# Where the squares of a norm, its scaling, its turns by feature halves, and the feed-forward sums stand in a two-block kernel

## The reference, cut to what matters

```
def rms_norm(x, g):
    y = xf * lax.rsqrt(jnp.mean(xf * xf, axis=-1, keepdims=True) + EPS)
    return (y * g.astype(jnp.float32)).astype(x.dtype)
...
# first block, every layer
h = _rms(x, norm_g[l]);  proj = h @ w_in[l]
dots = jnp.einsum('bqhd,bsd->bqhs', iqb, ik) * IDX_HD ** -0.5
score = jnp.einsum('bqhs,bqh->bqs', jax.nn.relu(dots), iwb)
...
x = x + merged @ w_out[l]
...
# second block, every layer
h = rms_norm(x, norm1) * (1.0 + scale1) + shift1
proj = h @ w_in
...
x = x + gate1 * mix
h2 = rms_norm(x, norm2) * (1.0 + scale2) + shift2
ff = jnp.square(jax.nn.relu(h2 @ w_ff1)) @ w_ff2
return x + gate2 * ff
```

## Time and profile before

| | |
|---|---|
| median of 3 executions | 2875.72 us (2864.07 to 2878.76) |
| profiled execution | 2862.72 us, span 2860.8 us |
| TensorE products busy | 2559.2 us, 89% of the span |
| VectorE / ScalarE / GpSimd busy | 1437.6 / 945.9 / 877.4 us |
| mean granted TensorE clock | 0.947 of full speed |

### The profile page before, as it was taken

How to read it: one execution, slowest core, us unless ns; L and a number is a source line. 1 busy time by engine, 2 the same in 40 slices (tenths; PEclk the granted TensorE clock), 3 DMA queues, 4 the chain that set the end, 5 groups by cost and what they waited for, 6 DMA issues and landing times. The chain is left out here.

```text
span 2860.8 us, 34637 instructions
## 1 busy us (share of the span) xinstructions
PE 2559.2 (89%) x12407; PEld 2036.8 (71%) x12407; DVE 1437.6 (50%) x2989; ACT 945.9 (33%) x1725; POOL 877.4 (31%) x366
## 2 busy tenths in 40 slices
PE   5998999889999898988988778999997877899999
PEld 4786777677778686767876446878787654787877
DVE  4396343565449634365464555444557455533234
ACT  3333243432333324343233452322223354232221
POOL 2232423224323241423432002444433200244442
PEclk9898999999989999999999789999998888999999
DMA  4222423225422241413432002444433200223232
GB/s 139 73 82 59 143 71 112 65 62 171 134 74 85 78 142 50 125 45 96 173 97 70 1 1 59 140 133 147 151 124 91 66 1 1 59 89 103 89 96 80
DMA packets 133583, 256.01 MB, mean 89 GB/s; under 512 B 23406, under 2 KB 30124, under 8 KB 133420
## 3 DMA queue, kind: packets, MB, share of 16 engines
q1 hardware_dynamic: 133420, 253.81, 28.4%
HBM read 249.58 MB, written 4.19 MB: 89 GB/s over the span
## 5 line engine op out<-in xcount | busy, mean ns | idle before, releaser
L693 POOL TENSOR_TENSOR wl<-raw,wh 128x1024 fp32r<-128x1024 f32 (+2 forms) x362 | 877.2, 2427 | 1955.8 <-ACT wh L1070 1954.1
L763 PE MATMUL ps<-wh,hTh 128*128 128x512 f32 (+4 forms) x1664 | 668.5, 402 | 14.6 <-DVE hTl L1624 14.6
L1070 ACT ACTIVATE wh<-raw 128x1024 fp32r<-128x1024 f32 (+2 forms) x362 | 379.8, 1049 | 864.8 <-PE ps L763 444.5
L763 PE MATMUL ps<-wl,hTh 128*128 128x512 f32 (+4 forms) x1664 | 649.7, 390 | 0.0
L763 PE MATMUL ps<-wh,hTl 128*128 128x512 f32 (+4 forms) x1664 | 649.2, 390 | 0.0
L763 PEld LDWEIGHTS ps<-wh,hTh 128*128 128x128 f32 x1664 | 329.0, 198 | 85.3 <-issue 29.8
L763 PEld LDWEIGHTS ps<-wh,hTl 128*128 128x128 f32 x1664 | 328.1, 197 | 60.5
L763 PEld LDWEIGHTS ps<-wl,hTh 128*128 128x128 f32 x1664 | 329.1, 198 | 53.1
L717 PE MATMUL ps<-cf,arena 128*128 128x128 f32 x800 | 135.5, 304 | 136.1 <-DVE arena L1983 24.2
L763 PE MATMUL ps<-hTh,wh 128*128 128x512 f32 (+1 forms) x672 | 250.0, 372 | 6.3 <-DVE hTl L1624 5.1
L763 PE MATMUL ps<-hTh,wl 128*128 128x512 f32 (+1 forms) x672 | 248.9, 370 | 0.0
(11 more groups left out here) (265 smaller groups left out, 3297.5 us busy)
## 6 DMA issues: line engine op xcount, KB each, us to landing
raw<-in_w_in_dram SPq DMA_DIRECT2D x160, 512.0 KB, 3.6
raw<-in_w_ff_dram SPq DMA_DIRECT2D x128, 512.0 KB, 3.6
modw<-in_w_mod_dram SPq DMA_DIRECT2D x96, 512.0 KB, 4.6
raw<-in_w_br_dram SPq DMA_DIRECT2D x24, 512.0 KB, 3.7
raw<-in_w_out_dram SPq DMA_DIRECT2D x24, 512.0 KB, 3.7
xm<-in_x_dram SPq DMA_DIRECT2D x8, 512.0 KB, 4.6
raw<-in_w_out_dram SPq DMA_DIRECT2D x16, 256.0 KB, 3.9
raw<-in_w_in_dram SPq DMA_DIRECT2D x8, 408.0 KB, 3.2
```

What stands on the lines that cost most here:

```text
L693: pool.tensor_tensor(piece(wl, g % RING, u), piece(raw, g % RING, u), piece(wh, g % SPLIT, u).bitcast(F32), ALU.subtract)\
L763: last = pe.matmul(*args, start=(q == 0 and c == 0 and n_pass == 0), stop=(q == u["quarters"] - 1 and c == u["chunks"] - 1 and n_pass == 2))
L1070: act.activation(piece(wh, g % SPLIT, u), piece(raw, g % RING, u), ACT.Copy)\
```

## The change

It has these parts, all in one build:

1. In a norm head with sweeps in front, the squares of tiles 0 and 1 stand ahead of the first of the last four sweeps and no longer behind it.
2. ScalarE scales the even tile of a pair, VectorE only the odd one.
3. The two tiles of a pair are turned by feature halves: half 0 of both tiles through VectorE and ScalarE first, then half 1.
4. Results that went from PSUM to `scr` and were used from there stay in their PSUM bank (relu of the indexer, `mix`, `fu`, `br`), which is marked free one operation later or more.
5. The feed-forward's sum is multiplied by the gate at group 6 of 0 to 7 and added to `xm`, and group 7 is multiplied and added by itself: three operations a slice at group 6 and two at group 7, where it was one and three.
6. The bias of the attention is one or two `tensor_scalar` of one column each.
7. As `mod` steps avoid sweeps beside a norm head, nearly all of them move by one sweep.

```diff
-            line.extend(last[0:1] + stats(0) + last[1:3] + two("turn", 0) + last[3:4] + stats(1))
+            line.extend(stats(0) + last[0:3] + two("turn", 0) + last[3:4] + stats(1))
...
                 elif kind == "turn":
                     _, stage, t = step
-                    pe.wait_ge(dve_result, at("xn", stage, t))
+                    pe.wait_ge(act_result if t % 2 == 0 else dve_result, at("xn", stage, t))
...
+                elif kind == "scale":
+                    _, stage, pair = step
+                    act.wait_ge(dve_result, at("root", step))
+                    act.activation(xn[:, 0], xm[:, 2 * pair], ACT.Copy, scale=nsm[:, 3, 0:1])\
+                        .then_inc(act_result, mark(act_result, ("xn", stage, 2 * pair)))
...
-                    act.activation(scratch(("scr", step))[:, 0:WIDTH[t]], ps[:, bank_of.get(step, 0), 0:WIDTH[t]], ACT.Relu)\
-                        .then_inc(act_result, mark(act_result, ("relu", step), ("free", step)))
+                    b = ps[:, bank_of.get(step, 0), 0:WIDTH[t]]
+                    act.activation(b, b, ACT.Relu).then_inc(act_result, mark(act_result, ("relu", step)))
...
-                    dve.tensor_tensor(tmp, b, tmp, ALU.mult).then_inc(dve_result, mark(dve_result, ("relu2", i, s), free))
+                    dve.tensor_tensor(b, b, tmp, ALU.mult).then_inc(dve_result, mark(dve_result, ("relu2", i, s), ("free", key)))
                     dve.wait_ge(dve_result, now(dve_result))
                     dve.wait_ge(act_result, at("fh", i, s))
-                    dve.tensor_tensor(F[g % 2][1][:, idx, t0:t0 + n], tmp, F[g % 2][0][:, idx, t0:t0 + n].bitcast(F32), ALU.subtract)\
-                        .then_inc(dve_result, mark(dve_result, ("free", key), *([] if mode == "feat0" else [("f", l, g, idx)])))
+                    dve.tensor_tensor(F[g % 2][1][:, idx, t0:t0 + n], b, F[g % 2][0][:, idx, t0:t0 + n].bitcast(F32), ALU.subtract)\
+                        .then_inc(dve_result, mark(dve_result, free, *([] if mode == "feat0" else [("f", l, g, idx)])))
...
-                    if g < FF_GROUPS - 1:
+                    if g < FF_GROUPS - 2:
                         dve.tensor_tensor(acc, b, acc, ALU.add).then_inc(dve_result, mark(dve_result, free))
                         dve.wait_ge(dve_result, now(dve_result))
                         return
...
+                    if g == FF_GROUPS - 2:
+                        dve.tensor_tensor(b, b, acc, ALU.add).then_inc(dve_result, mark(dve_result))
+                        dve.wait_ge(dve_result, now(dve_result))
+                    dve.tensor_tensor(b, b, grow2[:, c * 512:(c + 1) * 512], ALU.mult).then_inc(dve_result, mark(dve_result))
...
+                    dve.wait_ge(dve_result, at("guess", step, 3, 0))
+                    dve.tensor_scalar(nsm[:, 3, 0:1], y[:, 0:1], -1.0 / 8192.0, None, ALU.mult)\
+                        .then_inc(dve_result, mark(dve_result, ("root", step)))
+                    t = 2 * pair + 1
+                    dve.wait_ge(dve_result, at("guess", step, 3, 1))
+                    dve.tensor_scalar(xn[:, t % 2], xm[:, t], y[:, 1:2], -1.0 / 8192.0, ALU.mult, ALU.mult)\
+                        .then_inc(dve_result, mark(dve_result, ("xn", stage, t)))
...
-                    key = ("scr", step)
+                    key = step
                     W = WIDTH[t]
                     dve.wait_ge(act_result, at("relu", step))
-                    r = scr[:, scr_slot[key], 0:W]
+                    r = ps[:, bank_of.get(step, 0), 0:W]
```

More of the change, by code:

```diff
@@ L355, in build @@
                 kind = u["name"]
-                if kind in ("bq", "bk", "cq", "ck", "bz", "cz", "gz", "ek", "eq") or kind[:4] in ("gate", "mix0", "mix1") \
-                        or kind[:2] == "fu" or kind[:3] == f"fd{FF_GROUPS - 1}":
+                if kind in ("bq", "bk", "cq", "ck", "bz", "cz", "gz", "ek", "eq") or kind[:4] == "gate" \
+                        or kind[:2] == "fu":
                     keys = [("scr", i, 2 * p), ("scr", i, 2 * p + 1)]
-        elif step[0] == "index" or (step[0] == "y_tok" and step[2] != "c"):
+        elif step[0] == "y_tok" and step[2] != "c":
             keys = [("scr", step)]
@@ L1428, in evacuate @@
                     dst = xm[:, idx, c * 512:(c + 1) * 512]
[L1429 removed]
                     dve.wait_ge(product, at("product", i, s))
                     dve.wait_ge(act_result, at("grow", l, 0))
[L1432 to L1435 removed]
+                    dve.tensor_tensor(b, b, grow[:, c * 512:(c + 1) * 512], ALU.mult).then_inc(dve_result, mark(dve_result))
                     dve.wait_ge(dve_result, now(dve_result))
[L1437 to L1438 removed]
+                    dve.tensor_tensor(dst, b, dst, ALU.add)\
+                        .then_inc(dve_result, mark(dve_result, free, *([("x", ("f", l), idx)] if c else [])))
                 elif name[:2] == "fu":
@@ L1596, in _ @@
                                 .then_inc(dve_result, mark(dve_result, ("guess", step, r + 1, k)))
-                    for k in range(2):
-                        t = 2 * pair + k
-                        dve.wait_ge(dve_result, at("guess", step, 3, k))
-                        dve.tensor_scalar(xn[:, t % 2], xm[:, t], y[:, k:k + 1], -1.0 / 8192.0, ALU.mult, ALU.mult)\
-                            .then_inc(dve_result, mark(dve_result, ("xn", stage, t)))
+                    dve.wait_ge(dve_result, at("guess", step, 3, 0))
@@ L1603, in _ @@
                     _, stage, t = step
[L1604 removed]
+                    if t % 2 == 0:
+                        continue
                     for hb in range(2):
[L1606 to L1617 removed]
@@ L1618, in _ @@
-                    if t % 2 == 1:
+                        pair = []
                         for t2 in (t - 1, t):
                             st = ("turn", stage, t2)
-                            tile = slice(t2 * P, (t2 + 1) * P)
-                            for hb in range(2):
-                                dve.wait_ge(act_result, at("hh", st, hb))
-                                dve.tensor_tensor(hTl[:, 4 * hb:4 * hb + 4, tile], h32(st, hb),
-                                                  hTh[:, 4 * hb:4 * hb + 4, tile].bitcast(F32), ALU.subtract)\
-                                    .then_inc(dve_result, mark(dve_result, ("h", stage, t2, hb), ("free", (st, hb))))
+                            v = ps[:, bank_of.get((st, hb), 0)].rearrange("p (c n) -> p c n", c=4)
+                            pair.append((st, t2, v))
+                            dve.wait_ge(product, at("turned", st, hb))
+                            if stage[0] == "n":
+                                g = col("norm_g", stage[1], 4 * hb, 4).unsqueeze(2).to_broadcast([P, 4, P])
+                                dve.tensor_tensor(v, v, g, ALU.mult).then_inc(dve_result, mark(dve_result, ("h32", st, hb)))
+                            else:
+                                lo = (0 if stage[0] == "a" else 24) + 4 * hb
+                                g = gain[:, 0 if stage[0] == "a" else 1, 4 * hb:4 * hb + 4].unsqueeze(2).to_broadcast([P, 4, P])
+                                shift = modT[:, stage[1], lo:lo + 4].unsqueeze(2).to_broadcast([P, 4, P])
+                                dve.tensor_tensor(v, v, g, ALU.mult).then_inc(dve_result, mark(dve_result))
+                                dve.wait_ge(dve_result, now(dve_result))
+                                dve.tensor_tensor(v, v, shift, ALU.add).then_inc(dve_result, mark(dve_result, ("h32", st, hb)))
@@ L1627, in _ @@
+                        for st, t2, v in pair:
+                            tile = slice(t2 * P, (t2 + 1) * P)
+                            dve.wait_ge(act_result, at("hh", st, hb))
+                            dve.tensor_tensor(hTl[:, 4 * hb:4 * hb + 4, tile], v,
+                                              hTh[:, 4 * hb:4 * hb + 4, tile].bitcast(F32), ALU.subtract)\
+                                .then_inc(dve_result, mark(dve_result, ("h", stage, t2, hb), ("free", (st, hb))))
                 elif kind == "rstd":
@@ L1790, in _ @@
                     dve.wait_ge(dve_result, now(dve_result))
-                    dve.scalar_tensor_tensor(s[:, 2:2 + k], s[:, 0:k], -1.0, q_scale(m, t, h), ALU.mult, ALU.mult)\
-                        .then_inc(dve_result, mark(dve_result, ("bias", l, m, n)))
+                    for c in range(k):
+                        ins = dve.tensor_scalar(s[:, 2 + c:3 + c], s[:, c:c + 1], -1.0, q_scale(m, t, h)[:, c:c + 1],
+                                                ALU.mult, ALU.mult)
+                    ins.then_inc(dve_result, mark(dve_result, ("bias", l, m, n)))
                 elif kind == "prob":
```

53 lines of the change are left out of this document (15 added, 38 removed).

## The result

| | before | changed |
|---|---|---|
| median | 2872.51 us (4 executions, 2864.07 to 2878.76) | 2845.07 us (4 executions, 2837.92 to 2848.93) |
| profiled execution | 2862.72 us | 2837.92 us |

The ratio is 0.991, with a 95% interval of 0.9881 to 0.9939: 26 us less, between 18 and 34. A later series of six executions of the same kernel gave 0.9928 (0.9903 to 0.9953), 21 us less. The forecast was 12.7 us less, a time of 2857.6 us; the median of 2845.07 lies outside its own range (2851 to 2865) and inside the whole one (2842 to 2877).

What follows compares the result with a forecast made beforehand. TensorE, busy 2559.2 of 2860.8 us, was taken to set the end. Heads -15.9, indexer +9.7, feed-forward -3.6 and smaller terms sum to -12.7 us, put on the mean 2870.3: 2857.6 us; own range 2851 to 2865, whole 2842 to 2877.

Steps and rivals of the forecast that it cites:

- rival 2: Whole kernel: fewer long waits mean fewer lower-clock sweeps, and less contention; 12 us more gain, 2845 us; chance 0.17.
- The heads: Six norm heads: TensorE's waits at transposes shrink by new timetables, n0 alone gets longer; -15.9 us in all.
- Halves take off another 1.7: Head a1: turning by feature halves saves another 1.7 us, part of that head's -7.8 us.
- ScalarE's wait for the root: Norm heads: it delays roundings of weight pieces by 4 us, but these are wanted later; costed at nothing.
- The indexer: Groups of four dots: the fourth waits until VectorE has read the first bank, not for ScalarE's relu; +9.7 us.
- The feed-forward: Behind each `fu`: the first rest gets faster but its bank is freed later; -0.27 in 14 places, -3.6 us.
- `fd6`: Feed-forward group 6: 16 more operations cost +0.5 us, only in layer 0; bank waits here would show the forecast wrong.
- Slower, by one operand in PSUM being held up: `fu` rests and dot groups: GpSimd holds up operations with one PSUM operand as with two in SBUF; 2891 us; chance 0.04.
- the rule that the prediction weighed: VectorE: a PSUM source costs 120 fixed cycles against 58, an estimated 3 us on the path; the prediction followed the rows instead.
- `mod`, "-2, +0.5": Attention: the 2.90 us step ahead of it runs a sweep earlier, -2 us; another comes before the first attention, +0.5.
- More gaps cost some clock: +1: Indexer's stretch: more gaps in TensorE's work cost some clock, +1 us.
- Bias and `br`, "-1.5": Attention: one-column bias operations and `br` sums with one PSUM operand save 1.5 us on the path (bounds 0 and -5).

Runs made afterwards that it cites:

- experiment 2: The kernel before with only the norm heads' parts (squares first, even tile on ScalarE, turns by halves) and the shift of the mod steps; ratio 0.9965.
- experiment 5: The kernel before with the heads' three parts and the gate at group 6, whose sums stay in PSUM; ratio 0.9919.
- experiment 6: The changed kernel with the turns tile by tile again (part 3 taken back); ratio to the kernel before 0.9892.
- experiment 1: The changed kernel with the indexer's relu going to SBUF again and marking the PSUM bank free; ratio to the kernel before 0.9889, median 2842.07 us.
- experiment 4: The changed kernel with the mod steps back at the sweeps where the kernel before had them; ratio to the kernel before 0.9941, median 2853.15 us.
- experiment 3: The kernel before with everything of the change but the heads' parts, the mod steps staying where they were; ratio 0.9984.
- experiment 12: The kernel before with the squares first (which moves the mod steps) and the gate at group 6, sums in PSUM; ratio 0.992, median 2840.56 us.
- experiment 9: The changed kernel with relu to SBUF, turns by halves only in a heads, ScalarE scaling only in f heads; ratio to the kernel before 0.9882, median 2831.01 us.
- experiment 7: The changed kernel with both tiles of a pair scaled by VectorE (part 2 taken back); ratio to the kernel before 0.9939.

## Why the forecast held, and where it was short

The direction is right and so are the places; the size is not. The gain is 21 to 26 us where 12.7 was forecast, and the median lies in the whole range near its lower end, on the 2845 that rival 2 had (chance 0.17). That it lies in the range is in part luck: only the width added for rival 2 reaches down to it. TensorE's waits fell by 6.9 us in the first trace and 8.7 in the second; the rest of the 24.8 and 15.9 us is mostly busy time of the same products, at a clock that the sum priced at +1.

**The heads: right, place by place.** The timetables gave -15.9 and the traces show -15.6 and -15.7, with no head but a0 off by more than a microsecond (in the first trace 12.0 us of it are waits, the rest is the time that the same products took). First transposes of n1, a0, f0, a1 and f1 wait 0 to 0.3 us; the second ones of a0, f0, a1 wait 4.44, 5.78 and 5.64 for ScalarE's scaling, and n0's stand at 41.68 (said: near 42). The bounds of ScalarE's scaling were 0.7 and 1.1, the choice 1.05; it took 1.15 to 1.16. That the evacuation is two operations a slice at a1 was a condition of the timetable, and experiment 2 shows that without it a1 gains nothing (+1.0), experiment 5 that with it a1 is 8.0 us shorter. "Halves take off another 1.7" is what experiment 6 shows in a1 (5.6 against 7.3). That ScalarE's wait for the root holds up nothing is right: no wait on `wl` or `wh` stands behind it.

**The indexer: right.** +9.7 was said, +9.1 and +9.3 came, in 16 waits of 0.2 to 0.9 us, and experiment 1 takes them away. VectorE's first operation took 0.75 us from PSUM and not 0.69: it is not of L1448's kind.

**The feed-forward: mechanism right, size 2 us short.** -0.27 a place is exact at the place that the rows showed (14 times 0.27 is 3.8, not the 3.6 of the sum). The net is -4.9 and not -3.1, since places with more than the 1.02 us of that row (1.78 and 2.18, now 1.09 and 1.05) gained more; the wait of 2.18 us was followed by a granted clock of 0.57, the 1.05 us by the full one. `fd6` cost 1.0 us in layer 0 and not 0.5, in a wait for a bank, which the prediction had named as a sign of being wrong; it is the only one of those signs that appeared.

**Slower, by one operand in PSUM being held up: wrong, as rated (0.04).** Its sum does not fit its words (1.5 + 1.7 a place in 14 places would be 45 us, the 24 is 1.5 a place and the lost 3.6), which changes nothing here. The rests are at 692 ns in the mean, and at 144.90 a GpSimd operation of 2.34 us lies over L1675, which takes 0.75 with one operand in PSUM; from SBUF the same operation took 2.09. This is the relief that the Trainium skill names ("SBUF — State Buffer", SBUF: two separate sides), and the runs agree. On the rule that the prediction weighed, the higher fixed cost of a PSUM source (the Trainium skill, "VectorE: DVE Perf Modes", the TRN2 errata), the clean pair is the weighted score of the indexer at 128x128, where nothing held it up: L1672 took 352 ns with both tensors in SBUF, L1678 takes 351 with one in PSUM, and not the 65 ns more that the prediction estimated from the rule's cycles; the measurement decides. (The prediction's own pair, L1448 and L1475, agrees at 691 and 692 ns.)

**The term that was mis-sized: `mod`, "-2, +0.5".** The step moved ahead of its sweep gave the 2 us of wait back, and as much again in sweeps that no longer run at the lower clock, and two more waits of that stretch are shorter than in experiment 4 (0.21 us for 1.58 near 581, 2.03 for 3.43 near 695; experiment 3, without the shift, has 1.95 at the last). Experiment 4 puts the whole at 4 to 9 us. "More gaps cost some clock: +1" has the wrong sign: the time lost to the lower clock in the sweeps fell by 9 us. The heads' waits of n1 and a1 fell by 2.6 and 5.6 us, and the stretches by 4.2 and 7.3.

**Bias and `br`, "-1.5": not measured apart.** TensorE's waits at L907 are 3.2 us in the kernel before and in experiments 2, 5 and 12, and 1.2 in every kernel with parts 4 and 6; a part comes back behind them (the wait for L1808, now L1816, is 19.1 us before and 20.6 after). The bias took 27.2 us of VectorE in 64 operations, 13 of which lasted over 0.5 us though the median was 160 ns; now it takes 20.2 us in 96, none over 0.22 us. So the mean of 516 ns was not the price of the two-column form as such. No experiment takes these parts alone.

**What rival 2 said (2845) came out, its reason only in part.** Fewer long waits went with fewer slow sweeps: TensorE has 43 waits of 2 us or more in both traces of the changed kernel and 49 in the kernel before, and lost 58 and 67 us in its sweeps. But experiments 6 and 9, with 288.9 and 271.9 us of waits, lost 67 as well, so the count does not follow from the waits alone. Nor is every such wait followed by the lower clock: the 2.35 us at f1's first transposes in the kernel before are not, the 2.18 us of a feed-forward group are; over that kernel it is 37 of 49. And the 6.4 us at 1600 to 1760 in the first trace were not there in the second.

**What stays open.** The two traces of one kernel are 8.7 us apart at the same waits, and the kernels of experiments 6 and 7, with 288.9 and 287.6 us of waits, have medians of 2839 and 2857. Whether such a difference belongs to the order of the work, to the chip or to the executions that were drawn, these runs do not settle; the executions of experiment 7 alone span 20 us. So of the 21 to 26 us, heads, dots, feed-forward and end account for 11 to 13 in the two traces, `mod` for 4 to 9, and the rest is not assigned.

## What to carry to other kernels

Lay out the timetable of the wait's own place, from the rows of that place, and write down which other part of the change it leans on: the sum of the heads held to a microsecond, but the heads alone and everything else alone gave 15 us and together over 20. Price a removed wait with what the clock does behind it, from the rows of that place: in the first trace 15.5 of the 24.8 us were not waits but busy time. Ask of every result kept in PSUM who now frees the bank; where TensorE takes banks in turn, a faster VectorE operation can still be the later release. And take a change apart after it has won: parts 1 and 5, with the shift of `mod` that follows from 1, gave as much as all seven, the relu in PSUM cost 9 us, and the kernel with the best median is one without it.

## What the runs showed of the hardware that was not expected

- One kernel, two profiled executions on two occasions, waits within 2 us of each other: 2837.9 and 2846.7 us. The largest differences are in attention stretches of some 160 to 230 us, where TensorE had a granted clock of 0.93 and 0.89, and of 0.87 and 0.84.
- At n1 and a1 the stretch shortened by more than the waits that went: 2.6 us of waits and 4.2 us of time, 5.6 and 7.3.
- A `scalar_tensor_tensor` of 128x512 took 980 ns in the mean with both tensors in SBUF and 751 ns with one in PSUM (14 operations each). The mean hides two kinds: twelve of the 14 took 750 ns from SBUF as well, and two took 2345 and 2358.
- A `tensor_scalar` of 128x256 took 354 ns from SBUF and 484 from PSUM, one of 128x512 beside a GpSimd operation 2.09 us from SBUF and 0.75 from PSUM (two operations of each kind). For this operation the place in PSUM paid only where GpSimd was at work.
